# A PEER slot's sum in four 64x64 quarters of TensorE, and its 128x64 diagonal made by ScalarE

## The reference

```python
def block(args):                      # xb (128, 1024), idb and gb (128, 128): 8 heads x 16 experts per token
    xb, idb, gb = args
    u = jnp.take(u_tab, idb, axis=0)  # one row of 1024 per token and expert
    v = jnp.take(v_tab, idb, axis=0)
    act = jax.nn.gelu(jnp.einsum('nkd,nd->nk', u, xb).astype(f32)) * gb
    return jnp.einsum('nk,nkd->nd', act.astype(v.dtype), v)
```

## Time and profile before

| | |
|---|---|
| median of 3 runs | 2990.7 us (2988.2 to 2991.11) |
| profiled execution: span, its only own time | 2989.7 us |
| TensorE busy | 2666.7 us, 89% |
| VectorE busy | 2159.7 us, 72% |
| ScalarE busy | 637.2 us, 21% |
| GpSimd busy | 990.5 us, 33% |
| moved by DMA | 1182.34 MB, mean 395 GB/s |

### The profile page before, as it was taken

The page is one execution under the profiler, slowest core; times in us unless marked ns, Lnnn a source line. Parts: engine busy times, 40 slices in busy tenths (PEclk is TensorE's granted clock), DMA queues, the critical chain, the costliest instruction groups (busy, mean ns, idle before and its releaser), DMA issues.

```text
span 2989.7 us, 35028 instructions
## 1 busy us (share of the span) xinstructions
PE 2666.7 (89%) x11992; PEld 2186.6 (73%) x11992; DVE 2159.7 (72%) x6678; ACT 637.2 (21%) x1699; POOL 990.5 (33%) x1028
## 2 busy tenths in 40 slices
PE   8999999899998888989998888989999887877787
PEld 6778888678887677877887776868787665555555
DVE  1248858787588978687688778778588777678565
ACT  3231311272113116101111215201211110102001
POOL 0013333333333333333333333333333343333332
PEclk9999999999999999999999999999999999999999
DMA  5369999999999999999999999999999999999998
GB/s 190 103 247 426 413 408 426 426 365 409 415 387 392 386 427 405 425 421 427 426 415 416 414 426 416 413 427 423 427 398 407 409 427 426 426 417 411 427 425 344
DMA packets 166802, 1182.34 MB, mean 395 GB/s; under 512 B 19408, under 2 KB 19936, under 8 KB 24032
## 3 DMA queue, kind: packets, MB, share of 16 engines
q0 software_dynamic: 147456, 1073.81, 86.8%
q1 hardware_dynamic: 19168, 106.31, 9.0%
HBM read 1177.95 MB, written 2.10 MB: 395 GB/s over the span
## 4 chain that ended last, share of the span: by engine, by line
PE 53%; DMA 26%; DVE 11%; issue 8%; ACT 1%; POOL 0%; DVEq 0%; SPq 0%; POOLq 0%; ACTq 0%
PE main_bank L337 35%; DMA main_ring<-in_uv,main_idi 26%; PE main_bank L375 9%; PE main_bank L373 5%; DVE main_diagonal L311 2%; DVE main_ring L297 1%; DVE main_pick L202 1%; PE main_bank L543 1%; DVE main_hid L297 1%; DVE main_idf L209 1%; DVE main_topi L162 1%; DVE main_work L154 1%; DVE main_pick L196 1%; PE main_bank L735 1%; DVE main_topi L156 1%
## 5 line engine op out<-in xcount | busy, mean ns | idle before, releaser
L337 PE MATMUL main_bank<-main_ring,main_diagonal 128*128 128x256 f32 (+1 forms) x8160 | 1989.8, 390 | 294.6 <-DVE main_diagonal L311 294.0
L337 PEld LDWEIGHTS main_bank<-main_ring,main_diagonal 128*128 128x128 f32 x8160 | 1536.7, 193 | 656.4 <-DVE main_diagonal L311 434.4
L297 DVE CUSTOM_DVE_ANT_0 main_ring<-main_ring,main_bank 128x1024 f32<-128x1024 f32 x1024 | 1247.8, 1219 | 619.6 <-DMA main_ring<-in_uv,main_idi 607.0
L280 POOL DMA_INDIRECT main_ring<-in_uv,main_idi x1024 | 990.3, 967 | 1977.8 <-PE main_bank L337 1751.1
L302 ACT ACTIVATE main_act_out<-main_hid 128x1 f32<-128x1 f32 x1024 | 206.5, 203 | 2164.8 <-DVE main_hid L297 2153.5
L311 DVE TENSOR_SCALAR main_diagonal<-main_ident,main_act_out,main_gate 128x128 f32<-128x128 f32 x1024 | 359.2, 351 | 21.0 <-ACT main_act_out L302 13.9
L375 PE MATMUL main_bank<-main_xT,main_w_block 128*128 128x256 f32 x1408 | 358.4, 381 | 1.9 <-ACT main_xT L408 1.9
L375 PEld LDWEIGHTS main_bank<-main_xT,main_w_block 128*128 128x128 f32 x1408 | 268.3, 191 | 38.9 <-ACT main_xT L408 2.3
L375 PE MATMUL main_bank<-main_xT_query,main_w_block 128*128 128x256 f32 x512 | 124.2, 379 | 0.9 <-ACT main_xT_query L408 0.9
L375 PEld LDWEIGHTS main_bank<-main_xT_query,main_w_block 128*128 128x128 f32 x512 | 96.6, 190 | 14.5 <-ACT main_xT_query L408 1.2
L302 ACT ACT_TABLE_LOAD x82 | 105.2, 1283 | 1.4
(11 more groups left out here) (196 smaller groups left out, 1206.7 us busy)
## 6 DMA issues: line engine op xcount, KB each, us to landing
main_w_block<-in_w_query SPq DMA_DIRECT2D x32, 1024.0 KB
main_w_block<-in_w_ab SPq DMA_DIRECT2D x24, 1024.0 KB
main_ring<-in_uv,main_idi POOLq DMA_INDIRECT x1024
main_w_block<-in_w_c_in SPq DMA_DIRECT2D x16, 1024.0 KB
main_w_block<-in_w_out SPq DMA_DIRECT2D x8, 1024.0 KB
main_w_block<-in_w_c_out SPq DMA_DIRECT2D x8, 1024.0 KB
main_att_bias<-in_att_bias SPq DMA_DIRECT2D x16, 256.0 KB
main_keys<-in_keysT SPq DMA_DIRECT2D x2, 1024.0 KB, 12.8
```

The lines of the kernel that those rows point to most:

```text
L280: nc.gpsimd.indirect_dma_start(self.ring[n % self.bufs], None, self.uv[p // NT], bass.IndirectOffsetOnAxis(self.choice.idi[:, p % 2, k:k + ...
L297: self.nc.vector.tensor_tensor_reduce(out=row, in0=row, in1=self.ps[:, 6:8], scale=1.0, scalar=0.0, op0=ALU.mult, op1=ALU.add, accum_out=s ...
L337: last = self.nc.tensor.matmul(self.ps[:, 4 + at // T, at % T:at % T + wide], self.diagonal[:, n % DIAGS], self.ring[n % self.bufs][:, D + ...
```

## The change

The diagonal matrix of 128x128 becomes one of 128x64: rows 0 to 63 hold the diagonal of tokens 0 to 63, rows 64 to 127 that of tokens 64 to 127. `sum_rows` multiplies it in four products of 64x64 weights and 512 columns: row half r (tokens 64 r to 64 r + 63) and column half a of the v row go to PSUM partitions 64 a to 64 a + 63 of bank 4 + r. So the sum lies in PSUM in another order, and `add` and `add_halves` bring it back with four, or two and two, instructions of 64x512 (`add_columns`). The diagonal is made by ACT right behind the GELU, in two instructions: the GELU's result times the gate (128x1, in place), then a constant 128x64 matrix of two stacked identities, loaded at the start, times that result. DVE has no part in it any more, and the order changes from "behind the next slot's dot" to "behind the own GELU". The waits for the gates and for the sum three slots back move to ACT with it. The room in SBUF shrinks by what the smaller diagonals free.

```diff
--- before.py
+++ after.py
@@ -82,12 +82,11 @@
         return self.stack.enter_context(self.nc.Block())
 
 
-ROOM = 48312
-
-
 BUFS = 7
 DIAGS = 3
 HALF = T // 2
+SIDE = P // 2
+ROOM = 48312 - DIAGS * SIDE
 
 
 class Room:
@@ -255,14 +254,14 @@
 
 
     def __init__(self, nc, s, choice, A, consts, bank, resid, scale, gain_rows, ring, room):
-        self.nc, self.choice, self.ident, self.ps, self.resid, self.scale = nc, choice, consts["ident"], bank, resid, scale
+        self.nc, self.choice, self.ones, self.ps, self.resid, self.scale = nc, choice, consts["diagonal"], bank, resid, scale
         self.uv, self.gain, self.ring = (A["uv0"], A["uv1"]), gain_rows, ring
         self.bufs = len(ring)
         self.hid = room.sb("hid", [P, HK])
         self.act_out = room.sb("act_out", [P, HK])
-        self.diagonal = room.sb("diagonal", [P, DIAGS, P])
-        (self.gain_in, self.x_there, self.dotted, self.gelued, self.placed, self.v_done, self.added) = (s.sem(f"e_{x}") for x in (
-             "gain_in", "x_there", "dotted", "gelued", "placed", "v_done", "added"))
+        self.diagonal = room.sb("diagonal", [P, DIAGS, SIDE])
+        (self.gain_in, self.x_there, self.dotted, self.gelued, self.placed, self.v_done, self.added, self.weighed) = (s.sem(f"e_{x}") for x in (
+             "gain_in", "x_there", "dotted", "gelued", "placed", "v_done", "added", "weighed"))
         self.half_done, self.half_added = s.sem("e_half_done"), s.sem("e_half_added")
         self.landed = [s.sem(f"landed{k}") for k in range(self.bufs)]
 
@@ -301,21 +300,32 @@
         act.wait_ge(self.dotted, p * HK + k + 1)
         self.nc.scalar.activation(self.act_out[:, k:k + 1], self.hid[:, k:k + 1], ACT.Gelu_apprx_tanh).then_inc(self.gelued, 1)
 
-    def place(self, dve, p, k):
+    def place(self, act, p, k):
         n = p * HK + k
-        dve.wait_ge(self.gelued, n + 1)
+        act.wait_ge(self.gelued, n + 1)
         if k % (2 * PK) == 0:
-            dve.wait_ge(self.choice.gated, p * self.choice.PAIRS + k // (2 * PK) + 1)
+            act.wait_ge(self.choice.gated, p * self.choice.PAIRS + k // (2 * PK) + 1)
+        weight = self.act_out[:, k:k + 1]
+        self.nc.scalar.activation(weight, weight, ACT.Copy, scale=self.choice.gate[:, p % 2, k:k + 1]).then_inc(self.weighed, 1)
+        act.wait_ge(self.weighed, n + 1)
         if n >= DIAGS:
-            dve.wait_ge(self.v_done, n - DIAGS + 1)
-        self.nc.vector.tensor_scalar(self.diagonal[:, n % DIAGS], self.ident[:], self.act_out[:, k:k + 1],
-                                     self.choice.gate[:, p % 2, k:k + 1], ALU.mult, ALU.mult).then_inc(self.placed, 1)
+            act.wait_ge(self.v_done, n - DIAGS + 1)
+        self.nc.scalar.activation(self.diagonal[:, n % DIAGS], self.ones[:], ACT.Copy, scale=weight).then_inc(self.placed, 1)
 
     def add(self, dve, p):
         dve.wait_ge(self.v_done, (p + 1) * HK)
-        rows = self.resid[:, p % NT].rearrange("p (a d) -> p a d", a=2)
-        self.nc.vector.tensor_tensor(rows, self.ps[:, 4:6], rows, ALU.add).then_inc(self.added, 1)
+        for a in range(2):
+            last = self.add_columns(p, a)
+        last.then_inc(self.added, 1)
         dve.wait_ge(self.added, p + 1)
+
+    def add_columns(self, p, a):
+
+        cols = slice(a * T, (a + 1) * T)
+        for r in range(2):
+            rows = self.resid[r * SIDE:(r + 1) * SIDE, p % NT, cols]
+            last = self.nc.vector.tensor_tensor(rows, self.ps[a * SIDE:(a + 1) * SIDE, 4 + r], rows, ALU.add)
+        return last
 
     def add_halves(self, dve):
 
@@ -323,20 +333,19 @@
         for a in range(2):
             if a:
                 dve.wait_ge(self.v_done, 2 * NT * HK)
-            half = self.resid[:, NT - 1, a * T:(a + 1) * T]
-            self.nc.vector.tensor_tensor(half, self.ps[:, 4 + a], half, ALU.add).then_inc(self.half_added, 1)
+            self.add_columns(2 * NT - 1, a).then_inc(self.half_added, 1)
 
     def sum_rows(self, pe, p, k):
         n = p * HK + k
         if k == 0 and p:
             pe.wait_ge(self.added, p)
         pe.wait_ge(self.placed, n + 1)
-        wide = T if k == 0 else BC
-        for a in range(D // wide):
-            at = a * wide
-            last = self.nc.tensor.matmul(self.ps[:, 4 + at // T, at % T:at % T + wide], self.diagonal[:, n % DIAGS],
-                                         self.ring[n % self.bufs][:, D + at:D + at + wide], start=k == 0, stop=k == HK - 1 and at % T + wide == T)
-            if n == 2 * NT * HK - 1 and at + wide == T:
+        for a in range(2):
+            for r in range(2):
+                rows = slice(r * SIDE, (r + 1) * SIDE)
+                last = self.nc.tensor.matmul(self.ps[a * SIDE:(a + 1) * SIDE, 4 + r], self.diagonal[rows, n % DIAGS],
+                                             self.ring[n % self.bufs][rows, D + a * T:D + (a + 1) * T], start=k == 0, stop=k == HK - 1)
+            if n == 2 * NT * HK - 1 and a == 0:
                 last.then_inc(self.half_done, 1)
         last.then_inc(self.v_done, 1)
 
@@ -1275,7 +1284,8 @@
         gains = s.sb("gains", [P, 4, KD])
         ident = s.sb("ident", [P, P])
         iota = s.sb("iota", [P, P])
-        consts = {"ident": ident, "iota": iota}
+        diagonal = s.sb("ones", [P, SIDE])
+        consts = {"ident": ident, "iota": iota, "diagonal": diagonal}
         bank = s.ps("bank", [P, 8, T])
         room = Room(nc, s, ROOM)
         part = room.part
@@ -1322,6 +1332,7 @@
             mix0.sp_constants(sp)
             sp.dma_start(resid[:, 2:4], x[:, 2:4]).then_inc(loaded[1], 16)
             sp.dma_start(iota[:], A["iota"].partition_broadcast(P)).then_inc(loaded[1], 16)
+            sp.dma_start(diagonal[:], A["diagonal"]).then_inc(loaded[1], 16)
             tail0.sp_keys(sp)
             sp.dma_start(gain_rows[0], A["ffn_rows"][0].partition_broadcast(P)).then_inc(experts.gain_in, 16)
             for g in range(2):
@@ -1391,7 +1402,7 @@
                 tail0.act_gains(act, 0, i)
             tail0.act_squares(act, 0)
             norms.root_mean(act, 1)
-            act.wait_ge(loaded[1], 32)
+            act.wait_ge(loaded[1], 48)
             for t in range(2):
                 norms.squares(act, 2, mix0.rows[1], t)
             norms.root_mean(act, 2)
@@ -1406,6 +1417,7 @@
                 hf = 0 if p < NT else 1
                 for k in range(HK):
                     experts.activate(act, p, k)
+                    experts.place(act, p, k)
                     if p == 0 and k == 0:
                         norms.gains_in(act, 2, mix0.xT)
                     for q, at in sights(p, k):
@@ -1518,7 +1530,7 @@
             for n in (1, 2):
                 norms.mean_dve(dve, n)
                 norms.scale_dve(dve, n)
-            dve.wait_ge(loaded[1], 32)
+            dve.wait_ge(loaded[1], 48)
             choice.positions()
             experts.row_inputs(dve, 0)
             for i in range(2):
@@ -1537,10 +1549,6 @@
                     experts.dot(dve, p, k)
                     if p and k == 1:
                         experts.add(dve, p - 1)
-                    if k:
-                        experts.place(dve, p, k - 1)
-                    elif p:
-                        experts.place(dve, p - 1, HK - 1)
                     for q, at in sights(p, k):
                         for i in range(PH):
                             if at == HEAD_AT[q][i]:
@@ -1619,7 +1627,6 @@
                             final.mean_dve(dve, k // 10 - 1)
                         if k in (17, 27, 37):
                             final.dve(dve, k // 10 - 1)
-            experts.place(dve, 2 * NT - 1, HK - 1)
             experts.add_halves(dve)
             final.last_mean_dve(dve)
             final.last_dve(dve)
@@ -1756,6 +1763,7 @@
         "x": x["x"].reshape(T, D),
         "gains": np.stack([columns(x[n][k]) for n in ("mix_norm", "ffn_norm") for k in range(2)], axis=1),
         "ident": np.eye(P, dtype=np.float32),
+        "diagonal": np.tile(np.eye(SIDE, dtype=np.float32), (2, 1)),
         "iota": np.arange(P, dtype=np.float32),
         "scan_mask": (np.arange(HALF) % GCHUNK != 0).astype(np.float32),
         "causal": causal,
```

## The result

The changed kernel takes **2956.6 us** (median of 4 runs, 2952.3 to 2958.8); the kernel before took 2990.9 in the same comparison. The ratio is 0.9886, with a 95% interval of 0.9872 to 0.9900. The profiled execution's span went from 2989.7 to 2956.2 us, 33.5 less. The forecast was 2937, in a range of 2913 to 2970: the side and the range held, but 20 us of the expected gain are missing.

What follows compares the result with a forecast made beforehand. Transfers bound the kernel, at most 77 us to win; PE-full stretches 14.1, attention 6.2, bursts 14.5 and the rest 20.0 make 54.8, less 2 for additions 52.8: from 2989.7 to 2937 us, range 2913 to 2970.

Steps and rivals of the forecast that it cites:

- The bound and the mechanism: Over the slots, transfers bound the kernel; buffers held 2.8 us less put one more gather under way; at most 77 us.
- The quarters: TensorE's sum per slot: four quarters run at once, 0.86 us, or 1.16 us with weight pieces, against 1.73.
- second rival: In-order quarters keep a slot's sum at 1.73 us and shape changes add 0.3: slower, 3070 us; chance 6%.
- The diagonal: Made on ScalarE in each slot: 0.45 us of work, ScalarE's busy time rising to about 1100 us.
- VectorE's relief: Without the diagonals VectorE loses 359 us, 0.35 us a slot, and is busy near 1810 us.
- PE-full stretches: 420 to 440 and 820 to 940 us, TensorE full: 90% of 15.7 us regained, 14.1 us.
- Attention: 600 to 700 us, second half's attention between the slots: half of the lost 12.4 us regained, 6.2 us.
- Bursts: Three stretches with top-k or norm work: 80% of 18.1 us regained, 14.5 us, VectorE from 91% to about 77%.
- The rest: Short mixed dips spread over the slots: 65% of 30.8 us regained, 20.0 us.
- first rival: ScalarE becomes the pacemaker in the attention and recurrent gates; only 26 us won, 2964 us; chance 18%.
- The ends: One more load at the start and four additions behind the last sum at the end: 0 us.
- the additions: At seven stage boundaries, four adds of 64x512 in place of one: 11 us of VectorE, taken as 2 us lost.

Runs made afterwards that it cites:

- ring of 6: The changed kernel with six ring buffers instead of seven; 2977.2 us.
- no GELU tables: The changed kernel with a plain copy in place of the GELU, so that its table loads go; 2947.8 us.
- ScalarE's diagonal only: Against the kernel before: ScalarE makes the full 128x128 diagonal right behind the GELU, sums and additions as before; 2974.9 us.
- half-changes: Two kernels: the changed kernel with the 128x64 diagonal back on VectorE behind the next dot, 2971.0 us; the early ScalarE diagonal with the old sums, 2974.9 us.
- 5 diagonals: The changed kernel with five diagonal buffers instead of three, so ScalarE waits for the sum five slots back; 2954.2 us.
- hybrid: The changed kernel with VectorE making the diagonal behind the next dot in the attention's and recurrent gates' slots, ScalarE elsewhere; 2953.1 us.

## Why the prediction was right, and where it was short

- **The bound and the mechanism**: right. The bytes bound the kernel, the ring's release decides the dips, and a gather more is under way. The ring of 6 shows it.
- **The quarters**: right, 1.09 us with its fill for 0.86 and fill, and 1.1 us with shape changes for 1.16. All four quarters of a slot run beside each other, although a product's second record should stand ahead of the next quarter (the trace does not show the order in the program). The Trainium skill, page "TensorE: Matmul & The Clock Gate", section "Part 3: Packing small matmuls", has matmuls start and end strictly in order; by that a slot would be 1.73 us. The trace disagrees, and the second rival falls. (The 1.73 was too low for that rule: the first and the last record have nothing beside them, so it makes five steps of 0.43 us, 2.16.)
- **The diagonal**: a term mis-sized. ACT's 0.45 us a slot measured 0.294 + 0.348 = 0.64, and ACT is at 1287 us, not 1100. The forecast took the price of instructions without a per-partition scale. Such a scale costs about 0.09 us: in the run without GELU tables a plain copy of 128x1 takes 202 ns, and the gate's, with a scale, 294. The kernel before showed it too: copies of 128x256 from PSUM take 382 ns without one and 463 to 470 with one in its trace. The row was there and was not read.
- **VectorE's relief**: a term mis-sized, and a sign that did not come. DVE was to be near 1810 us and is at 1908. Each diagonal was counted as 0.351 us taken from DVE, 359 us in all. ScalarE's diagonal only, which leaves the additions alone, shows what it was worth: 2159.7 to 1897.4, 262 us, 0.26 a slot. The rest of the instruction had run beside the read of the dot's sum; in the kernel before both start at the same time:

```profile
2902.77 0.08 DVE L297 DVE_READ_ACCUMULATOR2_ANT main_hid<- 128x1 f32 x1
2902.77 0.34 DVE L311 TENSOR_SCALAR main_diagonal<-main_ident,main_act_out,main_gate 128x128 f32<-128x128 f32 x1
```

- **PE-full stretches**: 15.1 of 15.7 us regained, forecast 14.1. Right.
- **Attention**: the step that failed. "Half, 6.2" was a guess between nothing and all, and 0.2 came. The reasoning that ACT at 76 of 100 us is no full engine was true (78.5 measured) and not enough: the slots and the attention share ScalarE's queue there, and an engine need not be full to be late in a chain. In the half-changes the attention's slots take 133.7 us (quarters) and 142.8 (ScalarE's diagonal), before 136.9, together 137.5: a small gain, hardly above the scatter, and a loss that cancel. What was lost comes back, some 3 to 5 us, with 5 diagonals, with the hybrid or without the GELU's tables.
- **Bursts**: 7.9 of the forecast 14.5. The expected fall of DVE's load, from 91% to about 77%, is 0.35 us in a slot of 2.46; the 0.26 that were freed are 10 points, and at most 7 came: DVE is busy 91, 82 and 84% of the three stretches, where it was 93, 88 and 91. In 960 to 1020 us, where it hardly fell, a GELU still waits up to 6.5 us for its dot (7.4 before) and POOL up to 8.1 for a buffer (9.1 before):

```profile
POOL main_ring L279 <- PE main_bank L346: 44.0, 21, 8.1
ACT main_act_out L301 <- DVE main_hid L296: 34.9, 15, 6.5
```

The rest of what the diagonals left free, the burst's own instructions seem to have taken, since DVE starts the next of them as soon as it is free; that is a reading of the two profiles, and no run tested it. The length of the burst between two dots was to be read, and not DVE's share alone.
- **The rest**: 10 to 16 us for 20. The gates are in it, and there the first rival is right in stage 4 (404 to 394 GB/s, and a stage of 339.3 us for 338.1), though not in stage 2 (406 to 408). Relieving ScalarE shortens both.
- **The ends**: 0.8 us, not 0; **the additions**: too little to be told from 0 or from the 2 forecast.

Summed up, of the 19 us missing between 52.8 and 33.5: attention 6.0, bursts 6.6, the rest about 9.7 by the span; PE-full stretches give 1.0 back, and the 2.0 that the forecast took off for the additions go from the count too, since what they cost lies in the measured rest. Relieving ScalarE won at most 9 of them (no GELU tables, which also takes away loads that the kernel before had); the others lie in DVE's bursts and in what is left of the attention's chain, which no run took apart.

The first rival (2964, ScalarE as the pacemaker) came true in part of its places and the forecast in the others, and the time lies between the two, nearer to the rival: 7 us below 2964 and 20 above 2937. The 34 us won are just outside the 35 to 77 to which the prediction gave 67%. That the range held owes something to its taking in most of the first rival.

## What to carry to other kernels

In a kernel bound by a ring of transfers, count what is under way when a transfer lands; an earlier release and another buffer act on that same count, and taking one buffer away says in one edit whether it decides. Before work moves to an engine that is mostly idle, look for the stretches where it is not, and price the instruction by a row with the same operands, not by one with the same shape. An instruction taken away frees only the time in which nothing else of its engine ran: 0.26 us here for one of 0.35.

## What was not expected of the hardware

- A ScalarE copy with a per-partition scale costs about 90 ns more than one without: 294 ns for 128x1 where the GELU and a plain copy take 202, and 463 to 470 for 128x256 where it is 382.
- Half the partitions save VectorE nothing: 64x512 takes 688 ns in the additions, 128x512 was 0.70 us. The addition of 128x1024 was 1223 ns, so a quarter of its elements costs more than half of its time.
- With the sum at 1.09 us in place of 1.73, PE is granted a lower clock in the stages with slots alone, 0.64 in 2410 to 2600 us where it was 0.99; the levels are 1.2 and 2.4 GHz, and before it fell PE had 1.09 us of sums in each slot of 2.46. PE's busy time, 134 of 190 us there, is longer for that reason, and must not be read as load.
